# A two-layer mixture-of-experts trunk: one layout and one order of use for every expert weight unit

## What is computed

```
def expert_step(acc, ex):
    w_gu, w_d, g = ex
    a, b = jnp.split(xt @ w_gu, 2, axis=-1)
    return acc + ((jax.nn.silu(a) * b) @ w_d) * g[:, None], None

y, _ = lax.scan(expert_step, jnp.zeros_like(xt), (w_gate_up, w_down, gates.T))
```

## Time and profile before

| | us |
|---|---|
| median of 3 runs | 1149.8 |
| the three runs | 1147.35 to 1149.95 |
| the profiled execution | 1146.76 |
| its span, first to last instruction | 1145.0 |
| TensorE busy | 1050.3 (92%) |
| VectorE busy | 244.7 (21%) |
| ScalarE busy | 168.6 (15%) |
| transfers | 430.72 MB, mean 376 GB/s |

### The profile page before, as it was taken

One profiled execution on the slowest core, in us unless ns is written; L12 is line 12 of the kernel. 1 busy time (PEld: TensorE's weight loads), 2 busy tenths in 40 slices (PEclk: granted clock), 3 DMA queues, 4 the chain that ended last, 5 costly groups with the idle time before them and its releaser, 6 DMA issues.

```text
span 1145.0 us, 11474 instructions
## 1 busy us (share of the span) xinstructions
PE 1050.3 (92%) x4866; PEld 499.6 (44%) x4866; DVE 244.7 (21%) x520; ACT 168.6 (15%) x427; POOL 60.2 (5%) x94
## 2 busy tenths in 40 slices
PE   7999999989898979898999799999898989798988
PEld 6884542424242424242454655434333424242424
DVE  6993410101010100101035614101010101010101
ACT  3865200100000000000045402000000000000000
POOL 2980000000000000000000000000000000000000
PEclk9999899999999999999999998999999999999999
DMA  9793699999999999999995149999999999999996
GB/s 314 202 366 149 235 424 429 429 427 429 426 428 429 429 428 424 429 429 426 396 342 208 64 175 357 429 428 427 426 428 429 428 428 426 428 428 428 428 421 273
DMA packets 65006, 430.72 MB, mean 376 GB/s; under 512 B 12102, under 2 KB 22429, under 8 KB 44220
## 3 DMA queue, kind: packets, MB, share of 16 engines
q1 hardware_dynamic: 64830, 429.86, 91.0%
q10 hardware_dynamic: 126, 0.14, 0.0%
HBM read 428.94 MB, written 1.05 MB: 376 GB/s over the span
## 4 chain that ended last, share of the span: by engine, by line
PE 56%; DMA 39%; DVE 2%; ACT 1%; issue 1%; SPq 0%; ACTq 0%; DVEq 0%
DMA ring<-in_w_gate_up_dram 22%; DMA zone<-in_w_gate_up_dram 17%; PE bank L869 13%; PE bank L851 11%; PE bank L903 10%; PE bank L764 5%; PE bank L1066 2%; PE bank L804 2%; PE bank L994 1%; PE bank L918 1%; PE bank L1004 1%; PE bank L776 1%; PE bank L972 1%; PE bank L811 1%; ACT xT L624 1%; PE bank L978 1%
## 5 line engine op out<-in xcount | busy, mean ns | idle before, releaser
L869 PE MATMUL bank<-ring,zone 128*32 128x512 f32 x1184 | 334.5, 611 | 38.1 <-DMA ring<-in_w_gate_up_dram 25.9
L869 PE MATMUL bank<-zone 128*32 128x512 f32 x864 | 264.4, 610 | 26.8 <-DMA ring<-in_w_gate_up_dram 13.9
L869 PEld LDWEIGHTS bank<-ring,zone 128*32 128x32 f32 x1184 | 88.4, 112 | 220.3 <-issue 219.8
L903 PE MATMUL bank<-ring,xT 128*32 128x512 f32 x704 | 147.6, 594 | 4.6 <-ACT xT L624 4.6
L851 PEld LDWEIGHTS bank<-zone,xn 128*128 128x128 f32 x576 | 128.0, 313 | 15.3 <-issue 15.3
L869 PEld LDWEIGHTS bank<-zone 128*32 128x32 f32 x864 | 68.7, 112 | 145.2 <-issue 144.7
L851 PE MATMUL bank<-zone,xn 128*128 128x128 f32 x576 | 131.4, 387 | 0.3 <-DVE zone L1263 0.3
L1282 DVE TENSOR_TENSOR xT<-xT,bank 128x512 f32<-128x512 f32 x16 | 11.0, 688 | 464.2 <-PE bank L869 464.2
L903 PE MATMUL bank<-zone,xT 128*32 128x512 f32 x320 | 89.8, 594 | 2.8 <-ACT xT L624 2.8
L1287 DVE TENSOR_TENSOR h<-bank,h 128x512 f32<-128x512 f32 x64 | 44.3, 692 | 210.5 <-PE bank L918 210.5
L622 ACT ACTIVATE xT<-bank 128x512 f32<-128x512 f32 x16 | 9.6, 597 | 535.4 <-PE bank L869 535.4
(11 more groups left out here) (247 smaller groups left out, 630.1 us busy)
## 6 DMA issues: line engine op xcount, KB each, us to landing
ring<-in_w_gate_up_dram SPq DMA_DIRECT2D x74, 2048.0 KB, 35.2
zone<-in_w_gate_up_dram SPq DMA_DIRECT2D x54, 2048.0 KB, 35.3
ring<-in_w_down_dram SPq DMA_DIRECT2D x44, 2048.0 KB, 34.1
zone<-in_w_down_dram SPq DMA_DIRECT2D x20, 2048.0 KB, 35.4
ring<-in_a_pw_w_dram SPq DMA_DIRECT2D x8, 1024.0 KB, 12.0
ring<-in_a_pw_w_dram SPq DMA_DIRECT2D x2, 2048.0 KB, 11.2
ring<-in_w_o_dram SPq DMA_DIRECT2D x2, 2048.0 KB, 21.0
ring<-in_w_uq_dram SPq DMA_DIRECT2D x1, 2304.0 KB, 13.1
```

Source lines behind the costliest of these rows:

```text
L869: ins = nc.tensor.matmul(bank[b][s * CAP:(s + 1) * CAP, :], xs[:, k, s * CAP:(s + 1) * CAP], rhs[:, b * HALF:(b + 1) * HALF], start=(k == ...
L903: ins = nc.tensor.matmul(bank[2 + b][s * CAP:(s + 1) * CAP, :], hidT[:, k, s * CAP:(s + 1) * CAP], rhs[:, b * HALF:(b + 1) * HALF], start= ...
```

## The change

Every unit of every quad now has the block layout and is used in pairs: quad 0 of each layer (its twelve units, `gate_up`, `hidden_across`, `down`), the first `gather` of each layer, and the four `down` units of each layer's last quad. The convolution and the attention stay as they are. The amount of data and the number of matmuls are the same.

```diff
@@ -276,7 +276,7 @@
         def by_blocks(n):

-            return n != 0
+            return n >= 0

@@ -428,7 +428,7 @@
                             unit_free(e, i + (QUADS - 2), u + 6 if u < 2 else u, True)
-                        unit_dma(l, slot_last(l, u), u, (i + (QUADS - 1)) % QUADS * SIDE, u < GU)
+                        unit_dma(l, slot_last(l, u), u, (i + (QUADS - 1)) % QUADS * SIDE, True)
@@ -931,17 +931,17 @@
                 def quad(n, landed, first=False, end=False):

                     pe.wait_ge(e["xs_ready"], 2 * n + 2)
-                    gate_up(landed, not first)
+                    gate_up(landed, True)
                     gather(n + 1, True)
-                    hidden_across(n, not first and not end)
+                    hidden_across(n, True)
                     weights_back(n)
-                    down(n, landed, not first and not end)
+                    down(n, landed, True)
                     if first:
                         pe.wait_ge(rounds_ready, l + 1)
                     scatter(n, first)

                 pe.wait_ge(xn_ready, 2 * l + 4)
-                gather(0, False)
+                gather(0, True)
@@ -1289,7 +1289,7 @@
-                tokens_in(0, f"ffn_norm_g{l}")
+                tokens_in(0)
```

## The result

| | before | changed |
|---|---|---|
| median | 1149.51 us (4 runs, 1147.35 to 1149.95) | 1176.2 us (4 runs, 1174.27 to 1177.82) |
| ratio | 1 | 1.0243, 95% interval 1.0216 to 1.0270 |
| span of the profiled execution | 1145.0 us | 1174.6 us |

The changed kernel is 2.4% slower, by 26.7 us; the forecast was 1177.5 us, 27.7 us slower. The page of the changed kernel answers to the earlier trace rows: TensorE works 28 us more, the transfers move the same bytes in fewer packets, and the slices at the start of layer 0's mixture (155 in place of 235 GB/s in the fifth) show the longer pause.

A forecast was written before the change was run, and what follows sets the result against it. Transfers lead within a layer, TensorE at its ends; first gather 7.7, first release 10.6, last down 10.4 and longer pieces -1.0 sum to 27.7 us, moving the median from 1149.8 to 1177.5 us, range 1168 to 1184.

The forecast's parts named there:

- What bounds it: Within a layer transfers lead; TensorE's time counts before the first slot release and after the last landing.
- The first gather: Before each layer's first gate_up: the strided operand makes it slower, +3.84 us per layer, +7.7 in both.
- Rival (c): First gather: its stride costs nothing, giving 1170 us; chance 0.04.
- The first release: Quad 0's gate_up: first slots come free after 7.06 us, not 1.74; +5.32 us per layer, +10.6 in both.
- The rest of quad 0: After the first release: later slots come free in time, gate_up takes 24.1 to 26.0 us, nothing more is lost.
- rival (a): Quads 0 and 1: transfers lose rate with one or two units queued, 4 us a layer, about 1186; chance 0.12.
- Carrying through: From layer start to last landing: the late start persists, the last landing being 9.2 us later and no more.
- Rival (b): By the last quad something else leads, so the late start is lost and only last downs count: 1160; chance 0.06.
- (d): Transfers' total time alone sets the end, TensorE's order matters nowhere, all 32 units quicker: 1142; chance 0.03.
- The last down: Each layer's last quad: down takes 12.25 us instead of 7.07, +5.18 us per layer, +10.4 in both.
- The longer pieces: 16 KB instead of 4 KB pieces: only units 10 and 11 of each layer count, -1.0 us in all.

The follow-up runs named there:

- a gather twice: Two runs against the changed kernel: each layer's first gather repeated, 1189.78 us; the gather in quad 1 repeated instead, 1174.6 us.
- the wide gate_up: Changed kernel with quad 0's gate_up taking four experts at a time in the new layout, units released four together: 1177.13 us.
- the run with the stride alone: Kernel before with only the first gather strided and quad 0's gate_up rows in matching order, still four experts a unit: 1155.88 us.
- The run of pairs alone: Quad 0 in pairs with gate_up rows needing no stride, first gather unstrided, last down as in the kernel before: 1157.83 us.
- the run with short pieces: Changed kernel with every unit in four separate 4 KB rows per partition and no stride in gathers or transposes: 1203.54 us.
- the second comparison of medians: The changed kernel, unaltered, timed again against the kernel before on another chip: 1176.15 us, ratio 1.0255.
- quad 0 only: Changed kernel with the last quad's down put back to four-wide with 4 KB pieces; quad 0 and first gather stay changed: 1165.27 us.

## Why the prediction was right, point by point

**What bounds it.** That within a layer the landings lead and TensorE leads at the ends is shown by the pair of runs with a gather twice, +15 us against 0, and by the wide gate_up, which shortens TensorE's quad 0 by 8.7 us a layer and gains nothing.

**The first gather.** Forecast +3.84 us a layer from the row of the second gather; measured 7.72 against 3.82 us in layer 0's trace (7.33 in layer 1's), and +8.7 us (interval 5.6 to 10.9) for both layers in the run with the stride alone, forecast 7.7. Rival (c) is out.

**The first release.** Forecast 7.06 us into gate_up against 1.74 before; measured 7.10 against 1.98, both from the start of gate_up to unit 10's issue. The run of pairs alone gave +10.6 us, forecast +9.6.

The transfers, forecast to stand still until about 151.5, run again in the window from 150 (434 GB/s), after 82 GB/s from 146 to 150; the layer began 2.3 us earlier than forecast.

**The rest of quad 0.** A size that was off: four pairs in a row take 22.62 us, not 24.1 to 26.0, since each of the three seams saves time and not only the first (7.06 + 3 x 5.19). The forecast read 18.9 us for "three pairs without a wait" out of the earlier trace rows, and there is a wait in it: unit 17 of the kernel before was issued at 152.84 and landed 31.3 us later, at 184.1, and the third pair begins right behind it, at 184.25 and not at 182.8.

```profile
L409 SPq DMA_DIRECT2D ring<-in_w_gate_up_dram x1: 327/327/327, 152.8 to 152.8; - x1
...
DMA to landing us min/median/max: 31.3/31.3/31.3
```

It is off the path and changed nothing. TensorE then caught up sooner: a landing leads again in quad 2, at 226.73 + 32.63. The rate with a thin queue, rival (a), shows in windows of the changed kernel (last column GB/s):

```profile
150.00:152.00 2.00, 2.00 (x18) 0.60 (x18) 0.00 (x0) 0.00 (x0) 0.00 (x0) 1.00 1.01 434
...
173.00:183.00 10.00, 10.00 (x56) 2.79 (x54) 0.00 (x0) 0.00 (x0) 0.00 (x0) 1.00 1.01 431
...
160.00:200.00 40.00, 39.54 (x200) 16.89 (x196) 5.60 (x9) 2.63 (x5) 0.00 (x0) 1.00 1.00 426
200.00:240.00 40.00, 39.54 (x192) 16.80 (x188) 5.60 (x9) 2.93 (x7) 0.00 (x0) 1.00 1.01 430
```

From 150 to 152 only units 10 and 11 are issued and not landed, and from 175.4 to 178.9 three are. Neither stretch is slow, so (a) is out. One window of ten us, 193 to 203, has 419, which by the letter of the prediction is a dip below 420; the next has 434, and the 40 us around it the full rate.

**Carrying through.** The late start arrives at the last landing of both layers, 9.16 and 8.75 us for a forecast of 8.7. Rival (b), in which it would be lost on the way, is out; so is (d), since the first slot was not free as early as before.

**The last down.** Forecast +5.18 us a layer; the trace has 5.32 and 5.33 from the last landing to the scatter. The run with this part alone gave +11.8 us, forecast 10.4.

**The longer pieces.** The 1.0 us is too small to be seen by itself: in layer 0 the gather (+3.90) and the release (+5.12) make 9.02, and the stretch up to the last landing grew by 9.16, so no run shows this gain. Its price per unit, 0.24 us, was measured as 0.23 over 82 units in the run with short pieces.

**The number.** That the measured difference came within 1.0 us of the forecast is in part luck. In the two profiles the touched stretches give 28.6 us and the span 29.6, the second comparison of medians gave 29.5, and the four runs of the changed kernel spread over 3.6.

**What this leaves.** The change does bring its gain, a transfer rate 5% higher (429 against 410 GB/s from 695 to 700, where layer 1's first units load), but 28 of the 32 units that get it were off the leading stream, and it pays at both ends. Of the runs, none beats the kernel before; taking only the longer pieces, for quad 0's down units, would give some 1 us by the forecast's terms, below what can be measured, and was not tried.

## What to carry to other kernels

Where transfers lead, ask first what an edit does to the moment at which the first buffer comes free and to the work behind the last landing; in between TensorE had several us a quad to spend for nothing. A steady state's best form is not the best form for its first and last round: there a small unit of release, and all four column groups at work, were worth more than a 5% better transfer rate. A wait made to allow a faster form can take the clock along, so filling it is worth a try.

## What the runs showed of the hardware that I had not expected

The clock cost of a short wait. After 4.1 us without work, a down of 7.07 us took 9.91; with 3.7 us of work for nothing in the wait it took 7.07. A shorter wait costs the clock in one run and not in another (the attention, below).

The issue of a transfer can hold SyncE. In the last quad of layer 1, one of the 4 KB units of the kernel before kept its issuing instruction for 12.0 us and another for 5.9; none of the changed kernel's same four took more than 0.33. Line L409 in windows of the kernel before and of the changed one (ns min/median/max):

```profile
L409 SPq DMA_DIRECT2D ring<-in_w_down_dram x3: 383/384/12045, 1096.6 to 1097.8; - x3
```

```profile
L409 SPq DMA_DIRECT2D ring<-in_w_down_dram x4: 332/333/333, 1120.7 to 1122.4; - x4
```

It cost nothing here: the last down ran its 7.07 us without a wait. It goes with the piece. Issuing these four units took 18 to 20 us in layer 1 of every kernel that has them in 4 KB pieces (the one before, quad 0 only, stride only, pairs only, short pieces) and 2.0 us in the one with the last down alone and in the changed one. Whether the number of pieces (512 against 128 a unit) or their size does it was not tested apart.

Stretches that no edit touches differ by up to 4 us between kernels. Between layer 0's last scatter and layer 1's first gather the changed kernel took 3.35 us more, and its attention has a stretch at half clock that the kernel before does not have. The same two groups of instructions, before and then changed, take 2.9 us more, and windows over them have a granted clock of 1.00 before and 0.56 now (in the column before the DMA share):

```profile
649.83 2.07 PE bank L1055 x16
...
652.65 13.97 PE bank L1066 x32
```

```profile
661.99 3.28 PE bank L1055 x16
...
666.02 15.66 PE bank L1066 x32
```

```profile
650.00:655.00 5.00, 4.23 (x22) 2.88 (x23) 0.69 (x1) 3.08 (x12) 0.00 (x0) 1.00 0.00 0
```

```profile
665.00:670.00 5.00, 4.23 (x8) 1.77 (x7) 0.16 (x1) 4.52 (x17) 0.00 (x0) 0.56 0.00 0
```

In both kernels TensorE had waited 2.63 us for VectorE (L1449) just before, with the same work ahead of it. The same wait thus left the clock alone in one execution and halved it in the other; what decides is open.

From the first transposed tile of layer 1's attention to its first gather, the thirteen profiles took 125.5 to 129.3 us. And the convolution's first matmuls (L764) took 50.8 to 50.9 us in three of them (the kernel before, the last down alone, short pieces) but 48.61 in the ten others, with the same work there. It is not the clock: it was granted in full in that stretch with 50.92 us and with 48.61. Why is open.
